# expert_v in two parts: 896 columns multiplied densely with scattered weights, 1152 columns gathered

## The reference, cut to what matters

```python
eidx = jnp.take_along_axis(cidx, pos, axis=-1)        # 8 heads x 16 picked experts a token
gate = jax.nn.softmax(top, axis=-1)
...
u = jnp.take(expert_u, idx, axis=0)                   # idx = 128 * i1 + i2, KT = 128 a token
act = jax.nn.gelu(jnp.einsum('td,tkd->tk', h_t, u), approximate=False)
vv = jnp.take(expert_v, idx, axis=0)
return jnp.einsum('tk,tkd->td', g * act, vv)
...
return x + gate2 * rms_norm(ff, post_ffn_w)
```

## Time and profile before

| | |
|---|---|
| median of 3 runs | 2101.25 us (2100.34 to 2102.57) |
| span of the profiled execution | 2102.7 us |
| PE busy | 1749.5 us, 83% |
| DVE busy | 1404.0 us, 67% |
| POOL busy | 834.3 us, 40% |
| ACT busy | 377.9 us, 18% |
| moved by DMA | 681.05 MB, mean 324 GB/s |
| HBM read | 675.44 MB |

### The profile page before, as it was taken

How to read it: one execution, slowest core, us unless ns; L and a number is a source line. 1 busy time by engine, 2 the same in 40 slices (tenths; PEclk the granted TensorE clock), 3 DMA queues, 4 the chain that set the end, 5 groups by cost and what they waited for, 6 DMA issues and landing times.

```text
span 2102.7 us, 21519 instructions
## 1 busy us (share of the span) xinstructions
PE 1749.5 (83%) x7703; PEld 1326.7 (63%) x7703; DVE 1404.0 (67%) x2356; ACT 377.9 (18%) x778; POOL 834.3 (40%) x707
## 2 busy tenths in 40 slices
PE   3899999999999998999999999586888856566620
PEld 3788888888886547888888888474444423222210
DVE  6845566556655202588888875997787866766688
ACT  2022222222222102011111111342222201100000
POOL 2021322232223000256343444546777755655571
PEclk8899999999999999999999999677999988888865
DMA  9947545754575544589999999989999999999996
GB/s 395 407 143 270 223 148 203 262 216 168 211 265 195 227 153 160 203 322 410 409 409 407 409 407 409 344 296 368 421 422 421 421 422 421 423 422 421 422 422 277
DMA packets 122004, 681.05 MB, mean 324 GB/s; under 512 B 13488, under 2 KB 13616, under 8 KB 65840
## 3 DMA queue, kind: packets, MB, share of 16 engines
q0 software_dynamic: 73728, 419.46, 49.5%
q1 hardware_dynamic: 47760, 257.97, 32.0%
q10 hardware_dynamic: 416, 2.25, 0.3%
HBM read 675.44 MB, written 4.19 MB: 323 GB/s over the span
## 4 chain that ended last, share of the span: by engine, by line
PE 37%; DMA 36%; DVE 18%; POOL 5%; issue 3%; ACT 1%; DVEq 0%; ACTq 0%; POOLq 0%
DMA arena<-in_expert_v,arena 19%; DMA arena<-in_u_rows,arena 15%; PE ps L911 14%; DVE arena L1605 7%; PE ps L960 5%; POOL arena L550 5%; PE ps L989 4%; PE ps L1244 3%; DVE arena L1657 3%; DVE arena L1311 2%; DVE ps L1613 2%; PE ps L1130 2%; PE ps L994 2%; DMA arena<-in_ada 1%; PE ps L1003 1%
## 5 line engine op out<-in xcount | busy, mean ns | idle before, releaser
L1657 DVE SCALAR_TENSOR_TENSOR arena<-arena 128x2048 f32<-128x2048 f32 x179 | 420.8, 2351 | 125.8 <-DMA arena<-in_expert_v,arena 113.8
L550 POOL DMA_INDIRECT arena<-in_expert_v,arena x256 | 406.6, 1588 | 220.7 <-PE ps L1244 115.3
L1244 PE MATMUL ps<-arena 128*128 128x512 f32 x600 | 348.6, 735 | 168.0 <-DMA arena<-in_expert_v,arena 165.3
L550 POOL DMA_INDIRECT arena<-in_u_rows,arena x256 | 257.6, 1006 | 350.4 <-DVE arena L1605 291.2
L1204 PE MATMUL ps<-arena 128*128 128x256 f32 x1792 | 386.9, 379 | 0.0
L1204 PEld LDWEIGHTS ps<-arena 128*128 128x128 f32 x1792 | 340.4, 190 | 46.2
L1244 PEld LDWEIGHTS ps<-arena 128*128 128x128 f32 x600 | 134.7, 236 | 366.9 <-issue 341.9
L911 PE MATMUL ps<-arena 128*128 128x256 f32 x1440 | 339.3, 379 | 0.0
L1605 DVE SCALAR_TENSOR_TENSOR arena<-arena,ps 128x1152 f32<-128x1152 f32 x208 | 278.2, 1350 | 62.6 <-DMA arena<-in_u_rows,arena 60.0
L911 PEld LDWEIGHTS ps<-arena 128*128 128x128 f32 x1440 | 262.0, 190 | 29.4
L1230 PE MATMUL ps<-arena 128*128 128x128 f32 x512 | 128.0, 406 | 36.0 <-DVE ps L1613 33.4
(11 more groups left out here) (253 smaller groups left out, 1663.8 us busy)
## 6 DMA issues: line engine op xcount, KB each, us to landing
arena<-in_ada SPq DMA_DIRECT2D x96, 1024.0 KB, 5.5
arena<-in_u_dense SPq DMA_DIRECT2D x128, 448.0 KB
arena<-in_w_in SPq DMA_DIRECT2D x45, 1024.0 KB, 6.9
arena<-in_w_tail SPq DMA_DIRECT2D x32, 1024.0 KB, 7.0
arena<-in_w_in SPq DMA_DIRECT2D x12, 512.0 KB, 17.0
arena<-in_u_rows,arena POOLq DMA_INDIRECT x256
arena<-in_expert_v,arena POOLq DMA_INDIRECT x256, 26.3
arena<-in_x ACTq DMA_DIRECT2D x1, 2048.0 KB, 14.9
```

Source lines behind the costliest of these rows:

```text
L550: nc.gpsimd.indirect_dma_start(out=row, out_offset=None, in_=table[:, :], in_offset=bass.IndirectOffsetOnAxis(ap=i32(idx[:, b, k:k + 1]), ...
L1244: last = mm(bank(SUM_BANKS[b][c]), diag[(b * PE_ROWS[0] + m) % 2], v_row[n % len(v_row)][:, c * GROUP:(c + 1) * GROUP], start=(m == 0), st ...
L1657: stt(total[b], row, w, total[b], ALU.mult, ALU.add).then_inc(v_sum, 1)
```

## The change

expert_v is split as expert_u is: `v_dense` holds its first 896 columns, tiled by second key, and `v_rows` the other 1152. Only `v_rows` is gathered, into seven buffers of which six are the u rows' own, and all 256 rows are summed by DVE; the diagonal products are gone. For the dense part the weights of a token's picks are scattered over all 16384 experts: PE transposes each group's one-hot matrices (`turn_one_hot`), ACT writes them over the group's columns of `dense` (`keep_turned`), POOL (groups 0 to 31) or DVE (32 to 63) makes the one-hot of the second keys times the weights (`weigh`), PE multiplies the two (`token_weights`), and ACT writes the result over the same columns (`keep_weights`). When all 64 groups are done, PE multiplies `dense` with 128 tiles of `v_dense`, that SP loads into the buffers of the u tiles. Three constants change: `LATE` from 208 to 196, and `WEIGH_AT` = 232 and `LAG` = 6 are new. In the one-hot loop DVE makes at most one dot a group, over all 64 groups. `spread_keys` uses one bank instead of two. The end of the kernel works on the two parts apart.

The diff, cut to its core:

```diff
@@ sp
-            sp.wait_ge(y_ps, T // 4)
+            for j in range(NKEYS, 2 * NKEYS):
+                sp.wait_ge(tile_ps, j - 3)
+                sp.dma_start(u_tile[j % len(u_tile)].rearrange("p a b -> p (a b)"), v_dense[j - NKEYS]).then_inc(tile_land[j % len(u_tile)], 16)
@@ gpsimd
+            def weigh(q):
+
+                if q == 0:
+                    pool.wait_ge(wT_out, 1)
+                if q >= 2:
+                    pool.wait_ge(token_ps, q - 1)
+                for i in range(4):
+                    t = 4 * q + i
+                    nc.gpsimd.tensor_scalar(pick_w[q % 2][:, i, :], iota, idx2T[:, t:t + 1], wT[:, t:t + 1],
+                                            ALU.is_equal, ALU.mult).then_inc(pool_w, 1)
+
             for n in range(TB * KTOP):
...
                 if n >= UROWS:
                     pool.wait_ge(u_dot, n - UROWS + 1)
                 gather(u_row[n % UROWS], u_rows, b, k, u_land[n % UROWS])
+                if n >= WEIGH_AT:
+                    weigh(n - WEIGH_AT)
             for n in range(TB * KTOP):
                 b, k = divmod(n, KTOP)
                 if n == 0:
                     pool.wait_ge(tile_ps, NKEYS)
...
-                gather(v_row[n % len(v_row)], expert_v, b, k, v_land[n % len(v_row)])
+                elif n < len(v_row):
+                    pool.wait_ge(u_dot, TB * KTOP - UROWS + n)
+                else:
+                    pool.wait_ge(v_sum, n - len(v_row) + 1)
+                gather(v_row[n % len(v_row)], v_rows, b, k, v_land[n % len(v_row)])
+                if TB * KTOP - WEIGH_AT + n < P // 4:
+                    weigh(TB * KTOP - WEIGH_AT + n)
@@ scalar
+            def keep_turned(q):
+
+                act.wait_ge(turned, q + 1)
+                nc.scalar.activation(by_token(q), bank(7).rearrange("p (t k) -> p k t", t=4), ACT.Copy).then_inc(turn_out, 1)
+
+            def keep_weights(q):
+
+                act.wait_ge(token_ps, q + 1)
+                nc.scalar.activation(by_token(q), bank(token_bank(q)).rearrange("p (t k) -> p k t", t=4), ACT.Copy).then_inc(token_out, 1)
...
+            for q in range(T // 4):
+                if q == P // 4 + 3:
+                    gelu(0)
                 one_hot(q)
+                if q:
+                    keep_turned(q - 1)
+                if q > P // 4 + LAG:
+                    keep_weights(q - P // 4 - LAG - 1)
+            keep_turned(T // 4 - 1)
+            for q in range(P // 4 - LAG - 1, P // 4):
+                keep_weights(q)
+            gelu(1)
+            nc.scalar.preload_act_table_set("natural_log_exp_and_others")
+            for q in range(P // 4, T // 4):
+                keep_weights(q)
@@ tensor
+            def turn_one_hot(q):
+
+                pe.wait_ge(turn_out, q) if q else pe.wait_ge(idxT_out, 1)
+                for i in range(4):
+                    last = nc.tensor.transpose(bank(7, i * P, (i + 1) * P), hot[q % 2][:, i, :], ident)
+                last.then_inc(turned, 1)
...
+            def token_weights(q):
+
+                if q < P // 4:
+                    pe.wait_ge(pool_w, 4 * (q + 1))
+                    pe.wait_ge(token_out, q) if q else None
+                    pe.wait_ge(turn_out, q + 1)
+                else:
+                    pe.wait_ge(vec_w, 4 * (q - P // 4 + 1))
+                    pe.wait_ge(token_out, q - 1)
+                    pe.wait_ge(turn_out, q + 1)
+                for i in range(4):
+                    b, t = divmod(4 * q + i, P)
+                    last = mm(bank(token_bank(q), i * P, (i + 1) * P), dense[:, b, :, t], pick_w[q % 2][:, i, :], start=True, stop=True)
+                last.then_inc(token_ps, 1)
...
+            for q in range(T // 4):
                 if q + 1 < T // 4:
                     spread_keys(q + 1)
                 key_rows(q)
+                turn_one_hot(q)
                 if q == P // 4:
+                    turn_products(0)
+                if q == P // 4 + 3:
+                    turn_weights(0)
+                if q >= P // 4 + LAG:
+                    token_weights(q - P // 4 - LAG)
+            turn_products(1)
+            for q in range(P // 4 - LAG, P // 4):
+                token_weights(q)
+            turn_weights(1)
+            for q in range(P // 4, T // 4):
+                token_weights(q)
+            pe.wait_ge(token_out, T // 4)
+            for j in range(NKEYS):
+                s = (NKEYS + j) % len(u_tile)
+                pe.wait_ge(tile_land[s], 16 * ((NKEYS + j) // len(u_tile) + 1))
+                w = u_tile[s].rearrange("p a b -> p (a b)")
+                for b in range(TB):
+                    for lo, hi in ((0, GROUP), (GROUP, KU * P)):
+                        last = mm(sums(b)[:, lo:hi], dense[:, b, j, :], w[:, lo:hi], start=(j == 0), stop=(j == NKEYS - 1))
+                last.then_inc(tile_ps, 1)
@@ vector
             dve.wait_ge(idxT_out, 1)
+            for q in range(T // 4):
                 pick(q)
...
+                if q >= P // 4 or q % 4:
+                    dots(ndot[0], min(ndot[0] + 1, TB * KTOP))
+                    ndot[0] = min(ndot[0] + 1, TB * KTOP)
             dots(ndot[0], TB * KTOP)
+            activations(1)
+            add_row()
+            weights(1)
+            add_row()
+            keep_weights(1)
+            for q in range(P // 4, T // 4):
+                weigh(q)
+                if q % 3 == 2:
+                    add_row()
+            while nsum[0] < TB * KTOP - 2:
...
+                add_row()
+            gate_sums_of(1)
+            dve.wait_ge(fin_a, 2)
+            gate_sums_of(0)
+            while nsum[0] < TB * KTOP:
+                add_row()
+            gate_total(1)
+            finish(0)
+            finish(1)
@@ constants
-LATE = TB * KTOP - 48
+LATE = TB * KTOP - 60
+LAG = 6
+WEIGH_AT = LATE + 36
```

More of the change, by code:

```diff
@@ L100, in build_layer @@
 def build_layer(nc, x, cols, ada, w_in, w_tail, lora_up, keys,
-                u_dense, u_rows, expert_v, out):
+                u_dense, u_rows, v_dense, v_rows, out):
     with ExitStack() as ctx:
@@ L818, in _ @@
                 one_hot(q)
[L819 to L834, removed]
@@ new lines, in _ @@
+            act.wait_ge(gw2_ps, 1)
+            nc.scalar.activation(gw2[:, 0:3 * GROUP], ps[:, 2 * GROUP:5 * GROUP], ACT.Copy).then_inc(gw2_out, 1)
+            nc.scalar.activation(gw2[:, 3 * GROUP:], bank(7), ACT.Copy).then_inc(gw2_out, 1)
+            act.wait_ge(tile_ps, NKEYS + (D + GU) // P)
+            act.wait_ge(v_sum, KTOP)
+            square(total[0], 12, GU)
+            act.wait_ge(fin_a, 1)
+            act.wait_ge(tile_ps, 2 * NKEYS)
+            square(sums(0), 8, KU * P)
+            act.wait_ge(fin_a, 2)
@@ L837, in _ @@
+            act.wait_ge(gated, 2)
+            square(sums(1), 9, KU * P)
+            norm(0, 2)
+            act.wait_ge(v_sum, TB * KTOP)
+            square(total[1], 13, GU)
+            norm(1, 7)
         @block.tensor
@@ new lines, in turn_products, with turn_weights @@
+            def turn_products(b):
+                pe.wait_ge(picked_out, (b + 1) * P)
+                nc.tensor.transpose(bank(1 - b, 2 * P, 3 * P), val1T[:, b * P:(b + 1) * P], ident).then_inc(valT_ps, 1)
+            def turn_weights(b):
+                pe.wait_ge(wv_done, b + 1)
+                nc.tensor.transpose(bank(1 - b, 3 * P, 4 * P), wv[:, b, :], ident).then_inc(wT_ps, 1)
+            def token_weights(q):
[11 more added lines that the diff above has]
+                last.then_inc(token_ps, 1)
@@ L1258, in _ @@
                 key_rows(q)
+                turn_one_hot(q)
                 if q == P // 4:
[L1260 to L1271, removed]
+                    turn_products(0)
[18 more added lines that the diff above has]
+                last.then_inc(tile_ps, 1)
+                if j == D // P - 1:
+                    rows(gcol[:, 1, :], (2, 3, 4, 7)).then_inc(gw2_ps, 1)
         @block.vector
@@ L1631, in _, with activations @@
             ndot[0] = LATE
[L1633 removed]
+            def activations(b):
+                dve.wait_ge(u_dot, (b + 1) * KTOP)
                 dve.wait_ge(valT_ps, b + 1)
[L1636 removed]
+                tt(actv[:, b, :], bank(1 - b, 2 * P, 3 * P), actv[:, b, :], ALU.add).then_inc(act_done, 1)
             def weights(b):
@@ L1641, in weights, with keep_weights, weigh, add_row @@
                 tt(wv[:, b, :], wv[:, b, :], gate[:, b, :], ALU.mult).then_inc(wv_done, 1)
-                dve.wait_ge(wv_done, b + 1)
+            def keep_weights(b):
+                dve.wait_ge(wT_ps, b + 1)
+                V.tensor_copy(wT[:, b * P:(b + 1) * P], bank(1 - b, 3 * P, 4 * P)).then_inc(wT_out, 1)
+            def weigh(q):
+                if q == P // 4:
+                    dve.wait_ge(wT_out, 2)
+                dve.wait_ge(token_ps, q - 1)
+                for i in range(4):
+                    t = 4 * q + i
```

(18 more changed lines are left out.)

167 lines of the change are left out of this document (62 added, 105 removed).

## The result

The changed kernel takes 2311.93 us (median of 4 runs, 2310.3 to 2314.1) against 2101.91 before (now four runs): a ratio of 1.0996, 95% interval 1.0982 to 1.1009. It is 10% slower. The forecast was 2243 and its range ended at 2300: the direction and the mechanism were right, the size was not.

What follows compares the result with a forecast made beforehand. It took the last 640 us as bound by DMA bytes. Picks at 1331.1, group 38 at 1438, group 63 at 1670.5, dense product at 1751, plus 481 and 12.6, gave 2244.6, 2243 at the median; range 2115 to 2300.

Steps and rivals of the forecast that it cites:

- the chain: Groups 38 to 62: each group goes through all engines in a line, 9.5 us each, 24 periods, 228 us.
- the four tensor_scalars on POOL: POOL's weigh work in each group: 0.29 us apiece, 1.17 us for four, with ends 0.8 and 2.5.
- Start of the picks: First pick after the product stretch: 17.0 us sooner for moved dots, 4.5 us later for dense tiles, at 1331.1.
- Groups 2 to 38: One-hot loop: PE sets the pace at 2.8 us a group; key rows of group 38 end at 1438.
- Rest of the token weights: From group 63's end at 1670.5: 24.5 us to DVE's first weigh, then 56 us; dense product starts at 1751.
- Dense stretch: Dense product from 1751: transfers bind, 196 MB at 408 GB/s, 481 us; PE's 384 and DVE's 319 hidden.
- tail: After the last row lands at 2232: two adds, gate sums, finishes and the end, 12.6 us, to 2244.6.
- Strided loads: Rival on token_weights: strided weight loads are not hidden, 1.6 us more each, 99 us in all, 2342; chance 0.10.
- The second rival: Groups 38 to 62: POOL's part is covered, each period is PE's own 4.6 us, 118 us less, 2125; chance 0.10.
- The third: From the picks on: engine speed at full clock, byte saving decides, 2064 us, faster than before; chance 0.08.
- the turning point: Start of the dense product: it must come before 1609 for the kernel to be faster.

Runs made afterwards that it cites:

- the first experiment: The changed kernel with only WEIGH_AT changed, 232 to 228, so each weigh on POOL hangs on a dot four groups earlier: 2139.97 us.
- the third experiment: The changed kernel with weigh of groups 0 to 31 moved from POOL to DVE, one group ahead of its use: 2132.38 us.
- rows-early kernel: On top of the third experiment: late dots in groups 0 to 37, two v row sums in each of groups 38 to 63, gelu(1) and turn_weights(1) earlier: 2077.83 us.

## Why the prediction was wrong in size and right in kind

The step that failed is a term of the chain: the four tensor_scalars on POOL, put at 1.17 us with 2.5 as the upper end, took 3.14. It counts in 30 periods. With it alone put right the sum would have given about 2301; the other errors are smaller and partly cancel.

**Start of the picks**: forecast 1331.1, measured 1328.1: 3 us early.

**Groups 2 to 38**: forecast 2.8 us each, measured 2.44 (key rows at 1361.79 and 1364.23). PE had no gap and its clock was at full level in that stretch (1.00 from 1340 to 1400 us). Its weight loads:

```profile
1361.73 1.59 PEld L1265 LDWEIGHTS ps<-arena 128*128 128x128 f32 x8
...
1363.34 0.60 PEld L1272 LDWEIGHTS ps<-arena 128*128 128x128 f32 x4
...
1363.90 0.32 PEld L1253 LDWEIGHTS ps<-arena 128*128 128x128 bf16 x4
...
1364.18 1.60 PEld L1265 LDWEIGHTS ps<-arena 128*128 128x128 f32 x8
```

Key rows take 1.61 to the next load (forecast 1.70), the transposes 0.56 (0.5), the spread 0.28, where the forecast had 0.65. The 0.65 was read at 1346.5 us, soon after PE had stood idle for 17.5 us, and the granted clock was 0.51 there (1343 to 1350 us). Key rows of group 38 ended at 1424, 14 us ahead of the forecast. This error and that of the start had the opposite sign to the others.

**The chain**: its existence, its links, its place and its 24 turns were right, its period was not: 11.4 instead of 9.5 us. The term that was mis-sized is POOL's tensor_scalar. The prediction took 0.29 us from an affine_select of the same shape and allowed 0.62 at most; it took 0.79, so four took 3.14 instead of 1.17. No row of before showed a POOL instruction with operands read per partition, and "one input, same shape" was no bound for it. The trace of before had a warning that the earlier trace rows leaves out, an affine_select of half the columns that took more than twice the time (count, busy us, mean ns):

```profile
L472 POOL TENSOR_SCALAR_AFFINE_SELECT arena<-arena 128x64 f32<-128x64 f32 x1 | 0.7, 654 | 0.0
```

At 0.65 the upper end is 2.6 for four, still short of 3.14. The lower end was misworked: 0.8 instead of 1.17 takes 0.4 us off a period, not the 1.5 with which the range was drawn downwards. All other links agreed within 0.3 us and together take off 0.1: gather 1.03 for 0.94, token weights to spread 1.92 for 1.70, spread to key rows 0.43 for 0.65, wait to POOL 0.28 for 0.27. Group 63's key rows ended at 1701 instead of 1670.5.

**Rest of the token weights**: the same instruction again. POOL behind the loop:

```profile
1714.64 3.14 POOL L573 TENSOR_SCALAR arena<-arena 128x128 f32<-128x128 f32 x4
1717.94 1.03 POOL L557 DMA_INDIRECT arena<-in_v_rows,arena  x1 [0.17 <-issue]
```

Its six groups came 4.38 us apart (one 4.95), 1.03 + 3.14 and gaps, and not 2.7 as forecast from ACT's copy; that is 10 us. From DVE's first weigh to the dense product it took 65 us instead of 56: the row sums did not hide fully, PE waited 12 times, 5.5 us in all, for DVE's weighs. Dense product at 1800.5 instead of 1751.

**Dense stretch**: 408 GB/s were forecast and 407 measured while PE worked. PE's 128 tiles took 396 us, 3% above the 384 from the columns alone, hidden behind the transfers. Behind PE's end DVE sets the pace, and the rows alone come at 373 GB/s. From 2197 to 2298 us it waited for rows only this long:

```profile
DVE arena L1729 <- DMA arena<-in_v_rows,arena: 2.6, 7, 0.5
```

The sums are 1.50 us apart where dots back to back are 1.28 apart: an add takes 1.42 us, a dot 1.35, and each add is written to wait for the one before, whose total it adds to. The add has all inputs in the arena and the dot reads one from ps; no run separates what each of these differences costs. The prediction priced the add by the dot. Together with a tail of 14 us for 12.6 this is the last 18 us of the miss.

The row of the add in the kernel after (ns: min, median, max):

```profile
L1729 DVE SCALAR_TENSOR_TENSOR arena<-arena x254: 1407/1419/1479, 1734.1 to 2301.4; 128x1152 f32<-128x1152 f32 x127
```

So 2312.4 - 2244.6 = 68 us of miss are -3 - 11 (picks, first groups), about +45 (chain), +10 and +9 (behind the loop), +18 (dense stretch and tail).

**The rivals.** Strided loads: the load does get longer, as these two rows of the kernel after show (token weights, then key rows, whose stationary side is contiguous):

```profile
L1297 PEld LDWEIGHTS ps<-arena x512: 291/313/315, 1430.8 to 1799.3; 128*128 128x128 f32 x171
```

```profile
L1265 PEld LDWEIGHTS ps<-arena x512: 186/207/338, 1319.6 to 1700.7; 128*128 128x128 f32 x171
```

313 against 207 ns. But it stays nearly hidden: eight records start to next work in 1.92 us (1510.56 to 1512.48) where the key rows take 1.88, not 3.3. The longer load costs 0.04 us a group here. On the load the trace agrees with the rule on cachelines that the prediction took from the Trainium skill (Advanced Engine Details and Errata, section "SBUF Cachelines"): at a stride it is 0.1 us longer. The second rival, that the chain does not bind, is the first experiment's kernel: it gives 2140, for 2125 forecast. The third, faster than before: the turning point that the prediction set, a dense product before 1609, was drawn with the DMAs idle until then (and by the third experiment, which needs 511 us from there to the end, it would have been 1591). The rows-early kernel is faster with a start at 1655, because rows had been moved before it. The condition is on the bytes left at that moment, not on the moment.

## What to carry to other kernels

Where one engine's instruction is placed behind another's wait (here a weigh behind a gather that waits for a dot), count which iteration that wait belongs to: if it is the consumer's own, the iterations run through all engines in a line, and every nanosecond of every link counts once per iteration. A saving in bytes counts in full only where transfers run all the time; a buffer shared by two streams ties the second one's start to the first one's end. Price a new instruction by a row with the same kinds of operands, and where there is none take the range well beyond the nearest shape.

## What was not expected of the hardware

- POOL's tensor_scalar with two operands read per partition took 793 ns on 128x128 fp32 and 577 on 128x64, where POOL's affine_select on 128x128 took 293. DVE's took 342 (minimum 329) for the same work, four of them in 1.12 us. Whether POOL's time lies in the operands read per partition or in the two operations, no run separates.
- ACT's copy of 128x512 from ps with a stride of 512 bytes to groups of four in the arena took 597 ns, the same as the plain copy; the prediction had allowed 1.3 us.
- A weight load at a stride of 512 bytes took 313 ns (contiguous: 190 to 207) and stayed nearly hidden beside the stream of the pass before.
- In the chain, where PE stood idle for 6 to 7 us in every turn, its granted clock was 0.64 on the mean (from 1440 to 1450 us 0.50, the lower of its two levels, 1.2 GHz); in the first experiment, with the same products and no such waits, it was 1.00 (2.4 GHz). What that cost is bounded by rows: from token weights to the end of the key rows 4.4 us in the chain and 3.9 in the third experiment, so at most 0.5 us of the 11.4.
